# TensorE's loop over pairs 1 to 14, the last pair in single chunks, and the last norm's mean moved

## The reference

```python
x = x + parallel_mixer(rms_norm(x, norm_mix_g), w_in, ..., w_out)
x = x + memory_cross_attention(rms_norm(x, norm_xattn_g), rms_norm(mem, norm_mem_g), ...)
x = x + moe_ffn(rms_norm(x, norm_ffn_g), router_w, router_b, w_gate_up, b_gate_up, w_down, b_down)
return rms_norm(x, final_norm_g)

# moe_ffn, for each expert e, on the rows xb of the tokens that chose it:
gu = xb @ w_gate_up[e] + b_gate_up[e]          # (., 1024) @ (1024, 2048)
gate = minimum(gu[..., :1024], 7.0)
up = clip(gu[..., 1024:], -7.0, 7.0)
act = (up + 1.0) * gate * sigmoid(1.702 * gate)
y = act @ w_down[e] + b_down[e]                # (., 1024) @ (1024, 1024), scaled by the gate, added to x

# rms_norm
y = x * rsqrt(mean(x * x) + 1e-6) * g
```

## Time and profile before

| | us |
|---|---|
| median of 3 runs | 1188.1 |
| the profiled execution, its own time | 1185.88 |
| its span, from the first to the last instruction | 1184.2 |
| TensorE (PE) busy | 1106.1 |
| VectorE (DVE) busy | 350.5 |
| ScalarE (ACT) busy | 166.9 |
| DMA queue q1, share of 16 engines | 87.2% |
| DMA queue q8 (instructions) | 35 packets, 0.57 MB |

### The profile page before, as it was taken

How to read it: one execution, slowest core, us unless ns; L and a number is a source line. 1 busy time by engine, 2 the same in 40 slices (tenths; PEclk the granted TensorE clock), 3 DMA queues, 4 the chain that set the end, 5 groups by cost and what they waited for, 6 DMA issues and landing times.

```text
span 1184.2 us, 13896 instructions
## 1 busy us (share of the span) xinstructions
PE 1106.1 (93%) x5819; PEld 532.7 (45%) x5819; DVE 350.5 (30%) x740; ACT 166.9 (14%) x272; POOL 4.0 (0%) x23
## 2 busy tenths in 40 slices
PE   7999999999999999999898989898989898989897
PEld 6889886764434333433333333333334333333332
DVE  4685234463313212212121212222222213121313
ACT  3431234441101000010101010101010101010002
POOL 1000000000000000000000000000000000000000
PEclk9999999999999999999999999999989899999999
DMA  9842314677999999999999999999999999999995
GB/s 341 301 143 72 143 71 116 273 279 301 428 429 426 428 427 434 428 431 428 432 427 432 429 430 431 429 433 428 431 432 432 427 436 427 431 428 436 424 428 215
DMA packets 39029, 435.65 MB, mean 368 GB/s; under 512 B 5813, under 2 KB 5898, under 8 KB 20330
## 3 DMA queue, kind: packets, MB, share of 16 engines
q1 hardware_dynamic: 37066, 433.67, 87.2%
q10 hardware_dynamic: 1920, 1.34, 0.6%
HBM read 433.95 MB, written 1.05 MB: 367 GB/s over the span
## 4 chain that ended last, share of the span: by engine, by line
PE 58%; DMA 39%; DVE 1%; ACT 1%; issue 1%; SPq 0%; DVEq 0%; PEldq 0%
DMA ring<-in_w_down 35%; PE ps L2037 18%; PE ps L1997 14%; PE ps L1560 4%; PE ps L1671 4%; PE ps L1617 3%; DMA ring<-in_w_gate_up 3%; PE ps L2052 3%; PE ps L1540 2%; PE ps L1667 2%; PE ps L1728 2%; PE ps L1966 2%; PE ps L1804 1%; PE ps L1848 1%; DMA ring<-in_w_in 1%
## 5 line engine op out<-in xcount | busy, mean ns | idle before, releaser
L2037 PE MATMUL ps<-ring,work 128*64 128x512 f32 x1024 | 247.4, 633 | 38.6 <-DMA ring<-in_w_down 35.6
L1997 PE MATMUL ps<-ring,work 128*64 128x512 f32 x1024 | 225.6, 593 | 9.2 <-DMA ring<-in_w_gate_up 9.2
L1997 PE MATMUL ps<-work 128*64 128x512 f32 x1024 | 230.4, 592 | 0.2 <-DVE work L1396 0.2
L2037 PEld LDWEIGHTS ps<-ring,work 128*64 128x64 f32 x1024 | 81.0, 145 | 179.8 <-issue 163.4
L1997 PEld LDWEIGHTS ps<-ring,work 128*64 128x64 f32 x1024 | 71.2, 137 | 159.1 <-issue 140.7
L1997 PEld LDWEIGHTS ps<-work 128*64 128x64 f32 x1024 | 71.5, 137 | 136.7 <-issue 129.6
L1416 DVE TENSOR_SCALAR work<-ps 128x512 f32<-128x512 f32 x32 | 22.0, 686 | 197.7 <-PE ps L1540 197.7
L1439 DVE COPY work<-ps 128x512 f32<-128x512 f32 x16 | 11.1, 692 | 223.4 <-PE ps L1540 223.4
L1451 DVE COPY work<-ps 128x512 f32<-128x512 f32 (+1 forms) x16 | 11.1, 691 | 222.3 <-PE ps L2037 222.3
L2052 PE MATMUL ps<-work 128*128 128x512 f32 (+1 forms) x132 | 59.7, 608 | 10.4 <-ACT work L796 10.2
L1540 PEld LDWEIGHTS ps<-small,work 128*128 128x128 f32 (+1 forms) x354 | 44.8, 170 | 51.4 <-issue 45.4
(11 more groups left out here) (240 smaller groups left out, 728.3 us busy)
## 6 DMA issues: line engine op xcount, KB each, us to landing
work<-in_w_gate_up SPq DMA_DIRECT2D x64, 2048.0 KB, 36.5
ring<-in_w_gate_up SPq DMA_DIRECT2D x24, 4096.0 KB, 32.2
ring<-in_w_down SPq DMA_DIRECT2D x22, 4096.0 KB, 35.9
ring<-in_w_down SPq DMA_DIRECT2D x19, 2048.0 KB, 21.6
ring<-in_w_gate_up SPq DMA_DIRECT2D x16, 2048.0 KB, 20.2
ring<-in_w_in SPq DMA_DIRECT2D x7, 2048.0 KB, 15.9
ring<-in_xattn_w_kv SPq DMA_DIRECT2D x2, 2048.0 KB, 13.9
ring<-in_w_out SPq DMA_DIRECT2D x2, 2048.0 KB, 8.1
```

What stands on the lines that cost most here:

```text
L1997: last = nc.tensor.matmul(bank(b)[p], xg_T[k][:, kb, :], quad_columns(w[:, kk, D_MODEL * (q // 2):D_MODEL * (q // 2 + 1)], q % 2), start=F ...
L2037: last = nc.tensor.matmul(bank(Y_BANK + y)[p], act_T[k][:, b, HALF * c:HALF * c + HALF], w[:, b, 512 * q:512 * q + 512], start=False, stop ...
```

## The change

1. `by_halves` holds for all chunks of pair 15: chunks 1, 2, 5 and 6 are loaded as four single chunks where two twins were.
2. Of pair 15, chunks 9 and 10 are loaded in two parts of 1 MB and chunk 11 in four of 512 KB as before. The first parts count up the semaphores that the two loads of mem used at the start (renamed `mem_or_half_loaded0` and `1`), and TensorE waits for the first part before the first matmul and for the second before the third of four blocks.
3. TensorE's program unrolls only pair 0 and pair 15. Pairs 1 to 14 are five turns of a loop whose body holds three pairs; in the last turn the third is jumped over. `turned16` has a third entry, always 0, for the second places of twins: pairs 1 to 3 wait for them, and in later turns that wait is long satisfied.
4. `half_mean` of tile 1 stands on VectorE ahead of tile 0's adds, and `tile_root` of tile 1 on ScalarE ahead of tile 0's squares.

```diff
         def by_halves(i, c):
-            return i < BY_HALVES or (i == PAIRS - 1 and c >= 8)
+            return i < BY_HALVES or i == PAIRS - 1
...
+        def parts_of_last(c, s):
+            names = {9: ["mem_or_half_loaded0"], 10: ["mem_or_half_loaded1"],
+                     11: [f"piece_loaded{b}" for b in range(3)]}[c] + [f"slot_loaded{s}"]
+            n = SLOT // len(names)
+            return [(name, slice(n * j, n * j + n)) for j, name in enumerate(names)]
...
-            load_pair(last, last, lambda use: use, lambda use: use, range(8))
-            for c in (8, 9, 10):
+            for c in range(9):
                 load_half(last, c)
-            s, use, _ = chunk_place(last, 11)
-            sp.wait_ge(S(f"slot_free{s}"), use)
-            for b in range(4):
-                landed = S(f"slot_loaded{s}" if b == 3 else f"piece_loaded{b}")
-                sp.dma_start(place(s)[:, D_MODEL * b:D_MODEL * (b + 1)],
-                             half_rows(last, 11)[:, D_MODEL * b:D_MODEL * (b + 1)]).then_inc(landed, 16)
+            for c in range(9, PAIR_CHUNKS):
+                s, use, _ = chunk_place(last, c)
+                sp.wait_ge(S(f"slot_free{s}"), use)
+                for name, columns in parts_of_last(c, s):
+                    sp.dma_start(place(s)[:, columns], half_rows(last, c)[:, columns]).then_inc(S(name), 16)
...
             half_squares(1, 0, 1)
             half_squares(1, 1, 2)
+            tile_root(1, 1, 2)
             half_squares(0, 0, 3)
-            tile_root(1, 1, 2)
             half_squares(0, 1, 4)
...
                 for k, t in enumerate((1, 0)):
+                    if t == 0:
+                        half_mean(1, 1)
                     v.wait_ge(S("combine_filled"), 2 * PAIRS - 1 + k)
...
-            half_mean(1, 1)
             v.wait_ge(S("final_gain_loaded"), 16)
...
+            def kind_of_place(s):
+                return 1 if s >= RING else 2 if s in [second for _, second in TWIN_PLACES] else 0
+
             def chunk_landed(s, loads, turned16):
                 if loads is not None:
-                    pe.wait_ge(S(f"slot_loaded{s}"), turned16[s >= RING] + 16 * (loads + 1))
+                    pe.wait_ge(S(f"slot_loaded{s}"), turned16[kind_of_place(s)] + 16 * (loads + 1))
...
                 for b in range(4):
-                    if pieces and b < 3:
+                    if halves_of_load and b == 0:
+                        pe.wait_ge(S("mem_or_half_loaded1" if k else "mem_or_half_loaded0"), 32)
+                    if pieces_of_load and b < 3:
                         pe.wait_ge(S(f"piece_loaded{b}"), 16)
-                    elif pieces:
+                    if (halves_of_load and b == 2) or (pieces_of_load and b == 3):
                         chunk_landed(s, use, turned16)
...
-                for i in range(BY_HALVES):
-                    pair_of_experts(0, i, i, 2 * i + 1, 2 * i + 2, lambda c: first_pass_chunk(i, c), (0, 0),
-                                    opening=None if i else lambda: second_gather(0))
-                with pe.Fori(0, TURNS) as rev:
-                    turned16 = pe.snap(rev * (16 * TURN_USES)), pe.snap(rev * (16 * TURN_PAIRS))
-                    for q in range(BY_HALVES, BY_HALVES + TURN_PAIRS):
+                pair_of_experts(0, 0, 0, 1, 2, lambda c: first_pass_chunk(0, c), (0, 0, 0),
+                                opening=lambda: second_gather(0))
+                whole_turns = (PAIRS - 1) // TURN_PAIRS
+                with pe.Fori(0, whole_turns) as rev:
+                    turned16 = pe.snap(rev * (16 * TURN_USES)), pe.snap(rev * (16 * TURN_PAIRS)), 0
+
+                    def one_of_turn(q):
                         i = pe.snap(rev * TURN_PAIRS + q)
                         pair_of_experts(0, i, i, pe.snap(2 * i + 1), pe.snap(2 * i + 2),
                                         lambda c: first_pass_chunk(q, c), turned16)
-                for i in range(PAIRS - TURN_PAIRS, PAIRS):
-                    pair_of_experts(0, i, i, 2 * i + 1, 2 * i + 2, lambda c: first_pass_chunk(i, c), (0, 0),
-                                    final=(i == PAIRS - 1), pieces=(i == PAIRS - 1))
+                    one_of_turn(1)
+                    one_of_turn(2)
+                    with pe.If(rev < whole_turns - 1):
+                        one_of_turn(3)
+                i = PAIRS - 1
+                pair_of_experts(0, i, i, 2 * i + 1, 2 * i + 2, lambda c: first_pass_chunk(i, c), (0, 0, 0),
+                                final=True, pieces=True)
```

More of the change, by code:

```diff
@@ L432, in _ @@
                         sp.dma_start(mem_sb[:, t, :], mem[0, t * P:(t + 1) * P, :]) \
-                            .then_inc(S(f"mem_loaded{t}"), 16)
+                            .then_inc(S(f"mem_or_half_loaded{t}"), 16)
             def weight_rows(i, c):
@@ L1498, in expert_pass, with half_mean @@
                 return most
+            def half_mean(t, squared):
+                v.wait_ge(S("x3_squared"), squared)
+                nc.vector.tensor_scalar(half_bias[:, t:t + 1], half_ss[:, 2 * t:2 * t + 1], 1.0 / D_MODEL, EPS,
+                                        ALU.mult, ALU.add).then_inc(S("x3_bias"), 1)
             v.sem_inc(S("y_ready"), 1)
@@ L1516, in _ @@
                             .then_inc(S("x3_half"), 1)
[L1518 to L1521, removed]
             def scaled(t, columns):
@@ L2027, in down @@
                 s, use = chunk(8 + 2 * k + c)
-                if not pieces:
+                w = place(s).rearrange("p (k n) -> p k n", n=D_MODEL)
+                if not pieces or (k, c) == (0, 0):
                     chunk_landed(s, use, turned16)
-                w = place(s).rearrange("p (k n) -> p k n", n=D_MODEL)
+                    halves_of_load, pieces_of_load = False, False
+                else:
+                    halves_of_load, pieces_of_load = (k, c) != (1, 1), (k, c) == (1, 1)
                 for b in range(4):
-                    if pieces and b < 3:
+                    if halves_of_load and b == 0:
+                        pe.wait_ge(S("mem_or_half_loaded1" if k else "mem_or_half_loaded0"), 32)
+                    if pieces_of_load and b < 3:
                         pe.wait_ge(S(f"piece_loaded{b}"), 16)
-                    elif pieces:
+                    if (halves_of_load and b == 2) or (pieces_of_load and b == 3):
                         chunk_landed(s, use, turned16)
@@ L2077, in pair_of_experts @@
                 pe.wait_ge(S("act_T_ready"), n)
-                down(0, 0, chunk, turned16)
+                down(0, 0, chunk, turned16, pieces)
                 act_turned(1, m)
-                s = down(0, 1, chunk, turned16)
+                s = down(0, 1, chunk, turned16, pieces)
                 down_bias(1)
@@ L2083, in pair_of_experts @@
                 pe.wait_ge(S("act_T_ready"), m)
-                down(1, 0, chunk, turned16)
+                down(1, 0, chunk, turned16, pieces)
                 s = down(1, 1, chunk, turned16, pieces)
@@ L2125, in first_pass, with later_turned16 @@
                                         lambda c: first_pass_chunk(q, c), turned16)
-                for i in range(PAIRS - TURN_PAIRS, PAIRS):
-                    pair_of_experts(0, i, i, 2 * i + 1, 2 * i + 2, lambda c: first_pass_chunk(i, c), (0, 0),
-                                    final=(i == PAIRS - 1), pieces=(i == PAIRS - 1))
+                    one_of_turn(1)
[5 more added lines that the diff above has]
+                                final=True, pieces=True)
+            def later_turned16(done, i):
+                loads16 = pe.snap(done * 32 + 32 * i)
+                return loads16, 0, loads16
             def later_pass(r):
@@ L2135, in later_pass @@
                     pair_of_experts(r, i, pe.snap(r * PAIRS + i), pe.snap(r * E + 2 * i + 1),
-                                    pe.snap(r * E + 2 * i + 2), later_pass_chunk, (pe.snap(done * 32 + 32 * i), 0))
+                                    pe.snap(r * E + 2 * i + 2), later_pass_chunk, later_turned16(done, i))
                 i = PAIRS - 1
                 pair_of_experts(r, i, pe.snap(r * PAIRS + i), pe.snap(r * E + 2 * i + 1), pe.snap(r * E + 2 * i + 2),
-                                later_pass_chunk, (pe.snap(done * 32 + 32 * i), 0), final=True)
+                                later_pass_chunk, later_turned16(done, i), final=True)
             pe.sem_inc(S("act_T_filled"), 1)
```

3 lines of the change are left out of this document (2 added, 1 removed).

## The result

The changed kernel takes 1191.9 us in the median of nine runs (1189.8 to 1193.6); the kernel before, timed beside it, takes 1187.7 (nine runs, 1185.9 to 1188.5). The ratio is 1.0044, with a 95% interval of 1.0035 to 1.0052: slower, by 4.2 us in the medians and 5.2 by the ratio, where 3.9 us less were forecast. The profiled execution took 1193.4 us, its span 1191.7.

The account below looks back on a forecast made before the run. The unbroken stream of expert weights was taken as the bound, TensorE following it. Terms -1.5 + 0.1 - 2.0 - 0.45 = -3.85 us took the 1188.1 us median to 1184.2, range 1182.2 to 1187.0.

Parts of the forecast that it names:

- since that code is then resident: TensorE's loop: code of pairs 4 to 6, 13 and 14 needs no new fetch, so eleven fetches go.
- Fetches: Instruction queue q8: eleven fewer code fetches in the weight stream, which ends 2.0 us sooner.
- Single chunks: Pair 15: chunk 5 lands earlier without twins, TensorE 1.5 us sooner, less 0.1 for slower single loads.
- Parts: Last three down chunks of pair 15 in parts: earn nothing alone, guard 1.0 of the single loads' 1.5 us.
- The norm: Tail on VectorE and ScalarE: tile 1's mean and root moved earlier, scaling begins 0.45 us sooner.
- The sequencer: TensorE's loop jumps and exit: covered by waits and queued matmuls, bounds 0 to 0.5 us, taken as 0.
- Rival B: Last pieces of pair 15: the wait returns, about 1 of the 1.5 us is lost, 1185.2 us; chance 0.11.
- Rival C: TensorE's loop: code does not stay resident, every turn fetches it again, slower by 4.5 at 1192.6 us; chance 0.06.
- Net fetches: TensorE's loop if not resident: 28 fetches added where 11 went, net 17 at 0.18 us each, 3.1 us.
- The miss ahead of pair 15: TensorE's jump to pair 15 if the loop is not resident: misses for 3.3 us with no wait to hide it.

Follow-up runs that it names:

- e1: The changed kernel with TensorE's old loop put back, all other parts kept: 1187.4 us, ratio to before 0.9996.
- the padded kernel: The changed kernel with 66 tiny transposes (132 instructions) added at TensorE's start, which move its loop: 1184.7 us, ratio to before 0.9972.
- e8: The changed kernel with 33 tiny transposes (66 instructions) added at TensorE's start: 1199.9 us in one run.
- e2: The kernel before with only TensorE's new loop over pairs 1 to 14: 1194.9 us, ratio to before 1.0058.

## Why the prediction was wrong

**The step that failed** is "since that code is then resident" in the part on TensorE's loop. It rested on "the loop now jumps back over three pairs ... in 0.2 us", read as a statement about size, and the new loop has the same size within four instructions. Residence was decided by where the loop begins in a block of code: the old loop begins 0 to 47 instructions into its block, where up to 118 would do (7 x 256 - 1674), and the change moved the place by 127. Neither the instructions of a body nor the move of the loop was counted; both could be, from the kernel alone. What could not be read there is where in its block the old loop lay and how many blocks stay; that took the runs.

**The sum without that step** held. With the loop in a place where it stays, the changed kernel takes 1184.7 us (forecast 1184.2), and the ratio of 0.9972 is 3.3 us of gain against 3.85. The split is less sure than the sum: by the ratios all but the loop gave 0.4 (e1) where 1.85 was forecast, and the loop the other 2.9 where 2.0 was, though the profiles below are nearer to the forecast. Term by term:

- Fetches, forecast 11 fewer and 2.0 us: 10 fewer (25 against 35), and between the kernel with the old loop and the padded one 2.7 us in the medians (1187.4 to 1184.7) and 1.7 us in the stream losses (3.6 to 1.9). Right in kind and about in size (the 1.2 us for a fetch came from a share rounded to 0.3%; the packets themselves take 1.0 to 1.1); in the change as made it was +22 packets and +5.7 us of losses.
- Single chunks, forecast 1.4 net: the last 32 matmuls begin 5.78 us ahead of the last piece's landing (1178.65), 4.44 before (1169.36), so 1.34 sooner against the stream. Right in this profile; by the same sum it is 0.8 in e1 and 1.9 in the padded kernel.
- Parts, forecast as a guard of 1.0: 0.9 in the profile of the kernel without them; not seen in the medians.
- The norm, forecast 0.45: 0.45. Right.
- The sequencer, forecast 0: in the kernels whose loop stays, the If and the jump take 0.2 us and leave no gap. Right there; 6 to 7 us a turn otherwise.
- Rival B was in part real. In the padded kernel the last 32 matmuls touch the last piece:

```profile
1164.03 7.45 PE L2053 MATMUL ps<-ring,work 128*64 128x512 f32 x32
1171.63 4.23 PE L2068 MATMUL ps<-work 64*128 64x512 f32 x12 [0.16 <-PE ps L2053]
```

7.45 for 7.09, and 0.16 idle behind them: 0.5 us where 1 was named.

**Rival C** (0.06) is what happened, at 1192.6 against 1191.9. Its number is better than its terms. Net fetches were 22, not 17: against the padded kernel the four turns brought 32 packets and not 28 (nine in a whole turn, fewer in the last, which jumps over a body), and 10 went instead of 11. Each costs 0.21 us and not 0.18, so 4.6 us by that price, and 5.7 by the losses themselves, and not 3.1. The miss ahead of pair 15, put at 3.3 us, did not occur: the branch there took 0.24 us (the 237 of L2144), and only in e8, in another place, did it miss, for 6.5. Errors of opposite sign nearly cancel, so the closeness is luck. Its chance was too low. What stood against it, that as much code had fitted before, was no evidence for a loop in another place. The rule of the Trainium skill (Runtime: NRT & Kernel Launch, Instruction fetch mechanics) was set aside because its window of two pages disagreed with the trace; the same section's 2,048 instructions in blocks of 256 were the thing to work out, since 1,678 of 2,048 leave less than one and a half blocks.

Of the 7.5 us between the two spans, 2.9 are in the first 32 projection matmuls, where this execution of the changed kernel took 10.03 us against 7.14:

```profile
12.49 10.03 PE L1566 MATMUL ps<-work,ring 128*128 128x256 f32 x32 [2.06 <-DMA ring<-in_w_in]
```

The loads behind them start that much later, and the landings are still 3.7 us late at 474 us. The execution of before that was profiled was one of its shorter ones, this one of its longer; the medians, 4.2 us apart, don't rest on it.

## What to carry to other kernels

Before a loop is made or moved on TensorE, count its instructions and where it begins: with blocks of 256, one of 1,678 stayed when it spanned seven and was fetched again at every turn when it spanned eight, and 132 dummy instructions ahead of it were worth 7 us. After any change ahead of a loop, whatever it is for, look at the count of instruction packets and at the time of the jump back first; both show at once what the throughput strip hides. Under a saturated load stream an engine's stop may be free, once the loads are far enough ahead, while each 16 KB of code is not: about 0.2 us each here.

## What was not expected of the hardware

- A missed jump takes 5.9 to 7.3 us while the loads run at 430 GB/s, and 3.3 to 3.9 us at the end of the kernel when they are done (the last branch, in all thirteen profiles).
- A fetch of code costs the stream about 0.2 us, some three times the 0.07 us that its 1.1 us on one of 16 engines would be if shared out evenly, and at the end of the changed kernel half of the engines lagged by 8 to 11 us. Why the fetches weigh so unevenly is open.
- After a stop of 6 us in the changed kernel TensorE's granted clock in the next 16 matmuls was 0.56 to 0.71, and they took 4.99 to 6.29 us for 3.60 (4.67 to 6.29 over all kernels that miss). A stop of 3.2 us for weights did no less: 0.56 and 6.37 us in e1, 0.69 and 5.25 in the kernel before.
- The first projection matmuls took 10.03 us in the changed kernel's profile with a granted clock of 1.00. The clock, which was 0.80 where they took 8.83, doesn't explain that one, nor the 9.82 us at 1.00 in e2; its cause is open, as is that of the two clusters.
